# The S5 output matrix C of the second layer is turned before x, into the banks of the last output chunk

## The reference

```python
h = rms_norm(x, norm_g)
proj = h @ w_in                       # 10008 columns, split into the mixers' inputs, gates and merges
y = [rg_lru(...), s5(...), retention(...), nsa(...)]       # four mixers in parallel, 512 features each
branch = (y * silu(gate_paths)) @ w_branch                 # per mixer
x = x + sum(sigmoid(merge) * branch) @ w_out
```

```python
h[t] = a * h[t-1] + (f * B) u[t]                  # complex, per group; f from the parameters
y[t] = real(C h[t]) + d_skip * u[t]               # C given as s5_c_re and s5_c_im, (group, feature, state)
```

## Time and profile before

| | |
|---|---|
| median of three runs | 753.68 us (752.93 to 754.64) |
| the profiled execution | 753.15 us, its span 751.3 us |
| TensorE busy | 736.1 us (98%) |
| VectorE busy | 490.1 us (65%) |
| ScalarE busy | 418.9 us (56%) |
| GpSimd busy | 304.3 us (40%) |
| mean DMA rate | 169 GB/s |

### The profile page before, as it was taken

One profiled execution on the slowest core, in us unless ns is written; L12 is line 12 of the kernel. 1 busy time (PEld: TensorE's weight loads), 2 busy tenths in 40 slices (PEclk: granted clock), 3 DMA queues, 4 the chain that ended last, 5 costly groups with the idle time before them and its releaser, 6 DMA issues.

```text
span 751.3 us, 14575 instructions
## 1 busy us (share of the span) xinstructions
PE 736.1 (98%) x6014; PEld 624.7 (83%) x6014; DVE 490.1 (65%) x786; ACT 418.9 (56%) x673; POOL 304.3 (40%) x135
## 2 busy tenths in 40 slices
PE   7999999999999999999989999999999999999996
PEld 7988898889888888878888878988898788888885
DVE  4989977674587544535688799667564957153354
ACT  6885635548464655544558664454476445655441
POOL 3000000035778976688100000000645989766740
PEclk9999999999999999999999999999999999999998
DMA  8659646563444645555545865665624456545541
GB/s 257 176 182 286 202 152 221 173 195 113 140 135 148 197 142 143 169 169 169 149 95 168 282 190 171 200 202 186 197 86 139 141 169 176 169 141 163 176 130 56
DMA packets 87009, 126.85 MB, mean 169 GB/s; under 512 B 22072, under 2 KB 32672, under 8 KB 86944
## 3 DMA queue, kind: packets, MB, share of 16 engines
q1 hardware_dynamic: 86768, 125.89, 55.7%
q10 hardware_dynamic: 176, 0.04, 0.0%
HBM read 124.86 MB, written 1.05 MB: 168 GB/s over the span
## 4 chain that ended last, share of the span: by engine, by line
PE 86%; issue 7%; POOL 4%; DVE 1%; DMA 1%; SPq 0%; POOLq 0%; ACT 0%; DVEq 0%; ACTq 0%
PE proj L1723 63%; POOL w_lo L693 4%; PE M L1718 4%; PE proj L1760 4%; PE proj L1764 2%; PE proj L1791 2%; PE M L2118 2%; PE M L1920 1%; PE M L1888 1%; PE M L1931 1%; PE proj L1806 1%; PE M L2092 1%; PE proj L1822 1%; PE M L1995 1%; PE M L2087 1%
## 5 line engine op out<-in xcount | busy, mean ns | idle before, releaser
L693 POOL TENSOR_TENSOR w_lo<-raw,w_hi 128x1024 fp32r<-128x1024 f32 x112 | 287.8, 2600 | 399.3 <-ACT w_hi L715 376.2
L715 ACT ACTIVATE w_hi<-raw 128x1024 fp32r<-128x1024 f32 x200 | 206.4, 1054 | 112.2 <-PE proj L1723 58.5
L1723 PE MATMUL proj<-w_hi,h_hi 128*128 128x512 f32 x544 | 216.6, 398 | 1.5 <-POOL w_lo L693 1.5
L1723 PE MATMUL proj<-w_hi,h_lo 128*128 128x512 f32 x544 | 212.3, 390 | 0.5 <-issue 0.5
L1723 PE MATMUL proj<-w_lo,h_hi 128*128 128x512 f32 x544 | 211.9, 389 | 0.0
L1723 PEld LDWEIGHTS proj<-w_hi,h_hi 128*128 128x128 f32 x544 | 102.2, 188 | 23.6 <-issue 2.7
L1723 PEld LDWEIGHTS proj<-w_hi,h_lo 128*128 128x128 f32 x544 | 102.1, 188 | 22.7 <-issue 1.0
L1723 PEld LDWEIGHTS proj<-w_lo,h_hi 128*128 128x128 f32 x544 | 102.3, 188 | 20.4 <-issue 0.5
L1309 DVE TENSOR_TENSOR w_lo<-raw,w_hi 128x1024 fp32r<-128x1024 f32 x80 | 95.0, 1221 | 27.8 <-ACT w_hi L715 19.8
L1723 PE MATMUL proj<-w_hi,ys_hi 128*128 128x512 f32 x128 | 50.9, 397 | 0.5 <-POOL w_lo L693 0.5
L1723 PE MATMUL proj<-w_hi,ys_lo 128*128 128x512 f32 x128 | 50.0, 390 | 0.0
(11 more groups left out here) (337 smaller groups left out, 1171.3 us busy)
## 6 DMA issues: line engine op xcount, KB each, us to landing
raw<-in_w_in SPq DMA_DIRECT2D x152, 512.0 KB, 4.3
raw<-in_w_branch SPq DMA_DIRECT2D x32, 512.0 KB, 4.0
raw<-in_w_out SPq DMA_DIRECT2D x16, 512.0 KB, 4.5
raw<-in_s_w_glu SPq DMA_DIRECT2D x8, 512.0 KB, 4.5
raw<-in_w_in SPq DMA_DIRECT2D x8, 256.0 KB, 3.1
merged<-in_nsa_ck_w SPq DMA_DIRECT2D x4, 512.0 KB, 7.0
mt<-in_nsa_ck_w SPq DMA_DIRECT2D x4, 512.0 KB, 9.0
merged<-in_nsa_cv_w SPq DMA_DIRECT2D x4, 512.0 KB, 4.8
```

Source lines behind the costliest of these rows:

```text
L693: nc.gpsimd.tensor_tensor(w_lo[:, slot(s, l), 0:n * w], raw[:, u % N_RAW, 0:n * w], w_hi[:, slot(s, l), 0:n * w].bitcast(f32), ALU.subtrac ...
L715: i = nc.scalar.activation(out_, in_, func, **kw)
L1723: last = mm(dst, left[i], right[j], start=start and n == 0, stop=stop and n == 2, skip_group_check=True)
```

## The change

In layer 1 the transposes of C are issued between `last_chunk` and `turn_x` of layer 0's stream, four after `x_half` 2 and four after `x_half` 3, both behind `c_loaded` at 64, and write `proj[1]`, whose two banks held the two token tiles of `out_1b`. ScalarE's `keep_v0` reads from there and stands, in layer 1, before the wait for the end of chunk `u_s5`. TensorE waits for `v0_ready` before `cmp`, which overwrites `proj[1]`. Layer 0 keeps its order.

```diff
--- before.py
+++ after.py
@@ -570,6 +570,18 @@
             for half in range(2):
                 e = slice(512 * half, 512 * half + 512)
                 nc.vector.tensor_scalar(merged[:, t, e], x[:, t, e], st[:, 2 + t:3 + t], None, ALU.mult).then_inc(x_scaled, 1)
+
+        def turned_c(l):
+
+            return M[:, 0:2, :] if l == 0 else proj[1][:, :].rearrange("p (f n) -> p f n", f=2)
+
+        def turn_c(pe, l, f):
+
+            Layer(pe, l).wait_ge(c_loaded, 64)
+            for q in range(KB):
+                last = nc.tensor.transpose(turned_c(l)[:, f, q * P:(q + 1) * P], c_nat[:, f, q].rearrange("p g n -> p (g n)"), ident)
+            if f:
+                last.then_inc(cT_done, 1)
 
         def turn_x(pe, l, t):
 
@@ -833,7 +845,7 @@
                             for g in range(2):
                                 r = slice(64 * g, 64 * g + 64)
                                 run(v0[r, f].rearrange("p (b s) c -> p b s c", b=KB),
-                                    M[r, f, :].rearrange("p (b s g c) -> p b s g c", b=KB, s=4, g=2)[:, :, :, g, :],
+                                    turned_c(l)[r, f, :].rearrange("p (b s g c) -> p b s g c", b=KB, s=4, g=2)[:, :, :, g, :],
                                     ACT.Copy, v0_ready if f and g else None, scale=1.0 - 2.0 * f)
 
                     def spread_v(h):
@@ -862,13 +874,16 @@
                         run(y_s5[:, 2 * h:2 * h + 2, :].rearrange("p q (c i) -> p q c i", i=LC),
                             M[:, 1, :].rearrange("p (q i c) -> p q c i", q=2, i=LC), ACT.Copy, y_ready)
 
+                    if l:
+                        keep_v0()
                     next_cast("u_s5")
                     for e in range(LC):
                         keep_u(e)
                     run(u_s5[:, :, :].rearrange("p q (j c) -> p q j c", j=LC),
                         pr("u_s5")[:, :].rearrange("p (q c j) -> p q j c", q=KB, j=LC), ACT.Copy, evac("u_s5"))
                     spread_w(0)
-                    keep_v0()
+                    if l == 0:
+                        keep_v0()
                     trig(0)
 
                     act.wait_ge(chunk_done, ch("cmp"))
@@ -1856,15 +1871,6 @@
                         turn_x(tensor, 0, 1)
                     input_chunk()
 
-                    def turn_c():
-
-                        pe.wait_ge(hfull_done, KD)
-                        pe.wait_ge(c_loaded, 64)
-                        for f in range(2):
-                            for q in range(KB):
-                                last = tr(M[:, f, q * P:(q + 1) * P], c_nat[:, f, q].rearrange("p g n -> p (g n)"))
-                        last.then_inc(cT_done, 1)
-
                     def turn_w(h, f):
 
                         pe.wait_ge(wbd_ready, h + 1)
@@ -1932,7 +1938,13 @@
                                                   s5_h[:, f, s, :], start=False, stop=f == 1, skip_group_check=True)
                         last.then_inc(y_done, 1)
 
-                    turn_c()
+                    if l == 0:
+                        pe.wait_ge(hfull_done, KD)
+                        turn_c(tensor, 0, 0)
+                        turn_c(tensor, 0, 1)
+                    else:
+                        pe.wait_ge(hfull_done, KD)
+                        pe.wait_ge(v0_ready, 1)
                     if l == 0:
                         tensor.wait_ge(const_loaded, 16)
                     chunk("cmp")
@@ -2174,6 +2186,9 @@
                     last_chunk()
                     if l + 1 < DEPTH:
                         Layer(tensor, l + 1).wait_ge(vec_ready, 1)
+                        for f in range(2):
+                            pe.wait_ge(x_half, f + 2)
+                            turn_c(tensor, l + 1, f)
                         for t in range(TT):
                             turn_x(tensor, l + 1, t)
 
```

## The result

| | kernel before | changed kernel |
|---|---|---|
| median, 12 executions each | 753.03 us (752.15 to 754.64) | 755.29 us (753.76 to 757.08) |
| profiled execution | 753.15 us, span 751.3 | 753.76 us, span 752.0 |
| mean granted clock of the profiled execution | 0.997 | 0.997 |
| mean granted clock over timed executions | 0.9966 (35 executions beside e1) | 0.9946 (0.991 to 0.997) |

The ratio is 1.0025, with a 95% interval of 1.0017 to 1.0033: 1.9 us slower, 1.3 to 2.5. In its own profile the changed kernel is only 0.7 us longer; the profiled execution, 753.76 us, is the fastest of the twelve. The experiments ask first why the change loses time at all, and then what the slower executions have that this one hasn't.

What follows compares the result with a forecast made beforehand. TensorE, busy for 98% of the span, was taken to bound the kernel. Terms -0.87, +1.41 and nothing gave +0.54 us, which applied to the median 753.68 us made 754.2 us; range 752.7 to 756.0 us.

Steps and rivals of the forecast that it cites:

- the likeliest case: Whole kernel: C lands late and delays TensorE, +0.54 us net, 754.2 us, own range 753.9 to 754.6, chance 0.68.
- rival B: Border between layers: TensorE's 2.6 us hole lowers its clock, 1.7 us more, 755.9 us; chance 0.11.
- the stray of three executions: Whole-kernel measurement: a median of three may stray some 0.8 us either way, giving 753.0 to 755.4 us.
- Part 1: Before chunk cmp in layer 1: C's eight transposes leave TensorE's dense stretch, -0.87 us.
- Part 2: Before turn_x at the layer border: TensorE waits for C, landing at 379.77, delaying x and the input chunk, +1.41 us.
- Part 3: ScalarE's copies to v0 come earlier, ready 4.6 us before TensorE asks ahead of cmp; cost nothing.
- Rival A: Layer border: C lands in time and its eight transposes fit the holes, -0.87 us, 752.8 us; chance 0.09.
- the granted clock dips behind 380: Sign of being wrong: TensorE's granted clock falls after 380 us, just behind the layer border; no size given.
- Rivals C and D: C's load lands later, 754.8 or 756.0 us, chance 0.06; or something behind 426 absorbs the delay, 753.7 us, chance 0.06.

Runs made afterwards that it cites:

- e1: Changed kernel with layer 1's loads of C issued ahead of the four weight prefetches; 752.09 us against 752.87 of the kernel before, ratio 0.9988.
- e5: Changed kernel run again, unaltered, on a second chip; 754.63 us against 753.31 of the kernel before, ratio 1.0018.
- e11: Changed kernel with five blank products in the start of layer 0 and ten at the border; 752.92 us against 752.93 of the kernel before, ratio 1.0000.
- e3: Changed kernel with six blank products in TensorE's hole before the wait for C; 753.90 us against 752.87 of the kernel before, ratio 1.0013.
- e6: Changed kernel with ten blank products in TensorE's hole before the wait for C; 754.43 us against 753.31 of the kernel before, ratio 1.0014.
- e10: Changed kernel with five blank products in the start of layer 0; 755.66 us (5 executions) against 752.93 of the kernel before, ratio 1.0033.
- e2: Kernel before with only a wait for C's loads added ahead of turn_x in layer 1; 754.29 us against 752.87, ratio 1.0017.
- e4: Changed kernel with C's transposes put behind those of x; 752.98 us against 752.87 of the kernel before, ratio 1.0001.
- e8: Kernel before with C loaded ahead of the weight prefetches, C still turned before cmp; 753.04 us against 753.31, ratio 0.9996.

## Why the prediction was right, and where it was short

The forecast was +0.5 us and 754.2 us; measured were 755.29 us and +1.9 us (+1.4 in e5). The range held it, the likeliest case's own range (753.9 to 754.6) did not: the forecast's delay came, somewhat larger, and in some executions rival B on top. By the prediction's own line between same and slower, 755.2 us, the outcome was slower, to which it gave 0.18 against 0.77. That the range held has some luck in it: its top came from the stray of three executions and from parts of B and C, and it was built on a median of 753.68, where twelve executions gave 753.03. Moved down by that difference the range ends at 755.35, 0.06 us above what was measured.

- **Part 1, -0.87 us.** Right: e1 has it whole, -0.88 us of border and -0.9 us of time.
- **Part 2, +1.41 us.** The mechanism was right at every step that the first profile shows: C's transposes start at 380.02 (forecast 379.8), x follows without a hole, h_hi at 382.30 (382.1), the first product at 382.92 (382.7), `cmp` at 394.51 (394.2), the chunk is still 11.6 us. The size, as a difference of borders, was +0.54 us forecast for parts 1 and 2 together and came out at 0.50, 0.65, 0.71 and 1.04 us in the four profiles of the changed order without a fall (e11, e3, e6, and the first). The spread is C's landing against the end of layer 0: its transposes start 2.89 to 3.47 us after the start of the last output product (e5 and the first profile); forecast were 379.77 - 376.82 = 2.95, near the early end. I took one execution's distance between two engines' streams as fixed. The fit that the prediction takes from the Trainium skill (DMA: Bandwidth & Descriptors, the table of the two cost components) is given there for loads that GpSimd issues, while SyncE issues these; it gave an estimate of 2.3 us, and the last load of C took 2.7 to 3.1 us in the profiles with the late loads.
- **Part 3, nothing.** Right: slack 4.9 us for v0 (forecast 4.6), and e1 keeps part 3 without loss. wbd is done at 404.3 and is turned from 409.0.
- **Rival A** is what e1 built: -0.87 us forecast, -0.9 measured. In the changed kernel it never occurred.
- **Rival B** is the failed weight, and "the granted clock dips behind 380" was one of the signs of being wrong: it came in the profiles of e5 and e10. I gave it 0.11, since "the new hole is just under" the 2.7 us after which the clock fell at the end. That one fall doesn't tell which holes are safe: e5 fell with 2.5 us and the first profile didn't with 3.1, and in e2 the clock fell behind holes of 1.4 and 0.6 us, which most other profiles passed without a fall. The price of 1.7 us was about right: 1.3 us in e5, and in e10 2.39 us of border, of which 0.8 is the delay at its landing (its C starts 0.24 us later than forecast), so 1.6 us.
- **How often it fell** at the border is not counted; only the mean clock of each execution is there. It is under 0.997 in 18 of the 23 of the changed kernel and in 53 of the 89 of the kernel before, whose falls lie elsewhere, at least partly in the start of layer 0. With a delay of 0.5 to 1.0 us and 1.3 to 1.6 us for a fall, +1.4 and +1.9 us ask for a fall in about every second execution, if nothing else differs. That is worked out, not shown.
- **Rivals C and D.** The last load took 2.7 to 3.1 us from issue to landing, no more, in the profiles, so C showed in none of them. For D, from `cmp` to the last product layer 1 took 350.5 us before and 350.4 in the first profile, so nothing behind took the delay up. But over all 13 profiles this stretch runs from 349.7 (e11) to 351.8 us (e5), by "issue" holes and small ones, which the prediction has no term for.

## What to carry to other kernels

Work moved into a hole has to bring its inputs with it: look up when its load lands before moving it, and move the load as well (here the load alone gave nothing, the move alone lost 1.4 to 1.9 us, both together gained 0.9 us). On an engine that works in order, put what may be late behind what is ready. A hole on TensorE costs more than its length if the clock falls at it, which one profile may not show: look at more than one, and don't take the mean clock of an execution for a count of falls. Where blank work is put in as a control, compare the stretch behind it too: here e10 and e11 differ there by 1.5 us.

## What the runs showed of the hardware

- The granted clock can fall at a hole of 2.5 us and stay up at one of 3.1 us, in the same code. In e5 it fell about 1 us after work had begun again and stayed at half until near 384; in e2 it fell between 14 and 15 us and was back between 17 and 18 us.
- The same two holes at the start of layer 0, 1.4 and 0.6 us (1.38 and 0.60 in e2), passed without a fall in six profiles (before, the first, e1, e4, e5, e6) and had one in three (e2, e3, e8).
- Ten products of a blank tile in the hole at the border (2.4 us of work) went with no execution of 11 under 0.997 (e11), against 4 of 5 without them (e10).
- Between 440 and 456 us nine of the 13 profiles have a hole of TensorE of 0.18 to 1.23 us for which the profile names only "issue"; four have none (e2, e3, e8, e11).
